# A two-layer hybrid transformer with experts: first-layer expert rows are added to token rows in DRAM instead of by selection matmuls

## What is computed

```python
def expert_choice_ffn(h, w_router, w_gate, w_up, w_down):
    b, n, d = h.shape
    cap = CAPACITY_FACTOR * n // N_EXPERTS
    logits = jnp.einsum('bnd,de->ben', h, w_router).astype(jnp.float32)
    affinity = jax.nn.softmax(logits, axis=1)
    gates, idx = lax.top_k(affinity, cap)
    xs = jax.vmap(lambda hb, ib: hb[ib])(h, idx)
    a = jnp.einsum('becd,edf->becf', xs, w_gate)
    u = jnp.einsum('becd,edf->becf', xs, w_up)
    y = jnp.einsum('becf,efd->becd', jax.nn.silu(a) * u, w_down) * gates[..., None].astype(h.dtype)
    return jax.vmap(lambda yb, ib: jnp.zeros((n, d), yb.dtype).at[ib.reshape(-1)].add(yb.reshape(-1, d)))(y, idx)

# in each layer, after attention
xl = xl + gt_f * expert_choice_ffn(hl, ...)
if not last:
    xc = xc + cgt_f * expert_choice_ffn(hc, ...)
...
return rmsnorm(xl, g_final)
```

## Time and profile before

| | |
|---|---|
| median of three runs | 2272.16 us (2271.99 to 2275.36) |
| the profiled execution | 2279.44 us, span 2277.6 us |
| mean granted TensorE clock | 0.957 |
| TensorE busy | 2057.2 us, 90% of the span |
| VectorE, ScalarE, GpSimd busy | 823.4, 512.1, 124.7 us |
| DMA | 504.67 MB, mean 222 GB/s |

### The profile page before, as it was taken

The page is one execution under the profiler, slowest core; times in us unless marked ns, Lnnn a source line. Parts: engine busy times, 40 slices in busy tenths (PEclk is TensorE's granted clock), DMA queues, the critical chain, the costliest instruction groups (busy, mean ns, idle before and its releaser), DMA issues. The chain is left out here.

```text
span 2277.6 us, 27439 instructions
## 1 busy us (share of the span) xinstructions
PE 2057.2 (90%) x10742; PEld 990.3 (43%) x10742; DVE 823.4 (36%) x2126; ACT 512.1 (22%) x1192; POOL 124.7 (5%) x131
## 2 busy tenths in 40 slices
PE   5999999999988999999999899999999598887875
PEld 3445465655633333333333456455555233332322
DVE  3323256877650111130211431367776402020202
ACT  3211244544430010010100331154444101000001
POOL 1101000000001000000000010100000000000000
PEclk8999979999988999999999899999999799999998
DMA  8841200000079988889889302020003899999995
GB/s 333 304 147 51 55 20 1 1 1 1 19 301 426 405 347 349 354 332 397 339 320 375 114 19 74 1 75 1 1 1 148 340 426 426 427 427 426 427 427 224
DMA packets 87691, 504.67 MB, mean 222 GB/s; under 512 B 10163, under 2 KB 15197, under 8 KB 33293
## 3 DMA queue, kind: packets, MB, share of 16 engines
q1 hardware_dynamic: 82912, 487.00, 53.3%
q0 software_dynamic: 2880, 10.49, 1.3%
q10 hardware_dynamic: 1772, 5.43, 0.6%
HBM read 495.55 MB, written 7.34 MB: 221 GB/s over the span
## 5 line engine op out<-in xcount | busy, mean ns | idle before, releaser
L607 PE MATMUL psS<-arena 128*64 128x512 f32 (+9 forms) x4544 | 1171.8, 560 | 63.2 <-DMA arena<-in_w_up 23.9
L607 PEld LDWEIGHTS psS<-arena 128*64 128x64 f32 (+4 forms) x4544 | 464.0, 161 | 665.0 <-issue 603.5
L610 PE MATMUL psT<-ident,arena 128*128 128x128 f32 (+2 forms) x936 | 155.7, 296 | 68.3 <-DVE arena L1758 24.7
L1906 DVE TENSOR_TENSOR arena<-arena,psS 128x512 f32<-128x512 f32 x32 | 20.6, 684 | 514.7 <-PE psS L607 514.7
L1108 ACT ACTIVATE arena<-psS 128x128 f32<-128x128 f32 (+5 forms) x150 | 57.3, 412 | 581.0 <-PE psS L607 518.1
L610 PEld LDWEIGHTS psT<-ident,arena 128*128 128x128 f32 (+2 forms) x936 | 111.4, 148 | 156.5 <-issue 98.6
L1108 ACT ACTIVATE arena<-psS,nb 128x768 f32<-128x768 f32 (+2 forms) x200 | 159.0, 795 | 79.3 <-DVE nb L1749 77.9
L607 PE MATMUL psT<-arena 128*32 128x512 f32 x1536 | 174.7, 595 | 0.0
L1744 DVE TENSOR_REDUCE mx<-psS 128x1 f32<-128x768 f32 (+2 forms) x200 | 164.9, 824 | 22.9 <-PE psS L607 21.0
L1108 ACT ACTIVATE arena<-psT 128x512 f32<-128x512 f32 (+4 forms) x211 | 108.6, 517 | 225.6 <-PE psT L610 213.7
L607 PE MATMUL psO<-arena 128*64 128x128 f32 (+2 forms) x1600 | 153.2, 299 | 0.0
(11 more groups left out here) (221 smaller groups left out, 1484.9 us busy)
## 6 DMA issues: line engine op xcount, KB each, us to landing
arena<-in_w_gate SPq DMA_DIRECT2D x116, 1024.0 KB, 12.7
arena<-in_w_up SPq DMA_DIRECT2D x116, 1024.0 KB, 12.1
arena<-in_w_down SPq DMA_DIRECT2D x116, 1024.0 KB, 12.3
arena<-in_w_mod SPq DMA_DIRECT2D x40, 1024.0 KB, 9.0
arena<-in_w_in SPq DMA_DIRECT2D x6, 2048.0 KB, 7.9
gtb<-in_w_mod SPq DMA_DIRECT2D x8, 1024.0 KB, 7.2
normed_rows<-arena ACTq DMA_DIRECT2D x10, 512.0 KB, 13.4
arena<-in_w_out SPq DMA_DIRECT2D x8, 512.0 KB, 7.8
```

What stands on the lines that cost most here:

```text
L607: return nc.tensor.matmul(o, lhsT, rhs, start=start, stop=stop)
L610: return nc.tensor.transpose(o, in_, ident[0:n, 0:n])
L1906: last = V.tensor_tensor(ar[:, a:a + 512], ar[:, a:a + 512], bank(2 * g + h), ALU.mult)
```

## The change

In the first layer, the rows of quads 0, 1 and 2 are added to a DRAM copy of X, `summed_rows`; quad 3 and the whole second layer keep `combine`.

- VectorE writes, beside the indices for the gathers, a second form of the picked indices with one expert's rows per column (`idx`).
- SP stores X to `summed_rows` in the first quad, ahead of the first load of stage 6 (3 MiB), and loads it back in the last quad, ahead of the first load of stage 6, after it has waited for all additions.
- GpSimd issues for each of the three quads eight indirect transfers that add rows of `HID` to rows of `summed_rows`: for each expert its 64 latent rows, then its 32 context rows. Each latent one waits for the latent one before (`s_addl`), each context one for the context one before (`s_addc`). They stand ahead of the gather for the quad after next; those of the third quad stand after the last gather.
- ScalarE's silu for group 0 of quad q waits for two latent additions of quad q-1, that for group 1 for four, that for group 2 for the four context additions.
- `selection`, the high and low parts, `combine` and `combined` are left out for quads 0 to 2. The semaphores `yh`, `yl`, `st`, `ce` are counted over the combined quads alone. Three semaphores that were one per layer are shared by both (`mixed`, `Og`, `xg`), with counts that go on.

```diff
+COMBINED = ((NQ - 1,), tuple(range(NQ)))
+SUMS_STORED_AT, SUMS_LOADED_AT = 6, (NQ - 1) * NSTAGE + 6
...
+        sums = nc.dram_tensor("summed_rows", (NTOK, D), f32).ap()
...
+                    if l == 0 and n == SUMS_STORED_AT * QUAD:
+                        sp.wait_ge(z["xr"], TT)
+                        sp.dma_start(sums.rearrange("(t p) d -> p t d", p=P), X[:, :].rearrange("p (t d) -> p t d", t=TT)).then_inc(s_sum, 16)
+                    if l == 0 and n == SUMS_LOADED_AT * QUAD:
+                        sp.wait_ge(s_addl, 16 * QUAD * (NQ - 1))
+                        sp.wait_ge(s_addc, 16 * QUAD * (NQ - 1))
+                        load(X[:, :].rearrange("p (t d) -> p t d", t=TT), sums.rearrange("(t p) d -> p t d", p=P), s_sum)
...
+                def added(q):
+
+                    if q == 0:
+                        pool.wait_ge(s_sum, 16)
+                        pool.wait_ge(z["lgev"], 1)
+                    for e in range(QUAD):
+                        g, p0 = e // 2, e % 2 * CAP_L
+                        pool.wait_ge(z["y"], hidden_tile(l, q, g))
+                        if q or e:
+                            pool.wait_ge(s_addl, 16 * (QUAD * q + e))
+                        nc.gpsimd.indirect_dma_start(
+                            out=sums, out_offset=bass.IndirectOffsetOnAxis(ap=idx[0:CAP_L, q * QUAD + e:q * QUAD + e + 1], axis=0),
+                            in_=ar[p0:p0 + CAP_L, F["HID"] + g * D:F["HID"] + (g + 1) * D], in_offset=None,
+                            bounds_check=NTOK - 1, compute_op=ALU.add).then_inc(s_addl, 16)
+                        p0, c = e * CAP_C, NE + q * QUAD + e
+                        pool.wait_ge(z["y"], hidden_tile(l, q, 2))
+                        if q or e:
+                            pool.wait_ge(s_addc, 16 * (QUAD * q + e))
+                        nc.gpsimd.indirect_dma_start(
+                            out=sums, out_offset=bass.IndirectOffsetOnAxis(ap=idx[0:CAP_C, c:c + 1], axis=0),
+                            in_=ar[p0:p0 + CAP_C, F["HID"] + 2 * D:F["HID"] + 3 * D], in_offset=None,
+                            bounds_check=NTOK - 1, compute_op=ALU.add).then_inc(s_addc, 16)
+
                 for q in range(NQ):
                     if q == 0:
                         pool.wait_ge(z["want"], 2 * l + 1)
-                    elif q == 1:
-                        pool.wait_ge(z["gp"], KD)
+                    elif q == 1 or l == 0:
+                        if q > 1:
+                            added(q - 2)
+                        pool.wait_ge(z["gp"], KD * q)
                     else:
                         pool.wait_ge(z["ce"], (q - 1) * 2 * len(TILES[l]))
...
+                if l == 0:
+                    added(NQ - 2)
...
-                        if st == 0 and q:
+                        if st == 0 and q - 1 in COMBINED[l]:
                             combine(q - 1)
...
-                        if q:
+                        if q and wc and g < 2:
+                            act.wait_ge(s_addl, 16 * (QUAD * (q - 1) + 2 * (g + 1)))
+                        elif q and wc:
+                            act.wait_ge(s_addc, 16 * QUAD * q)
+                        elif q:
                             act.wait_ge(z["ce"], q * NC)
...
-                    for g in range(NX):
+                    for g in range(NX if q in COMBINED[l] else 0):
                         act.wait_ge(z["y"], hidden_tile(l, q, g))
...
+                            V.tensor_scalar(idx[0:CAP_L, 0:NE], bank(4, 0, CAP_L, 0, NE), float(CTX), None, ALU.add)
+                            link(V.tensor_copy(idx[0:CAP_C, NE:2 * NE], bank(4, 0, CAP_C, 32, NE)))
...
-                    dve.wait_ge(z["yh"], hidden_tile(l, q, g))
+                    if q not in COMBINED[l]:
+                        return
+                    dve.wait_ge(z["yh"], split_tile(l, q, g))
...
-                    if q:
+                    if q - 1 in COMBINED[l]:
                         combined(q - 1)
-                    selection(q)
+                    if q in COMBINED[l]:
+                        selection(q)
```

More of the change, by code:

```diff
@@ L365, in backbone_program @@
         s_g = [sem(f"first_rows{i}") for i in range(3)]
+        s_sum, s_addl, s_addc = sem("sums_moved"), sem("latent_rows_added"), sem("context_rows_added")
         s_xd, s_lgx, s_lgxc = sem("rows_stored"), sem("context_logits"), sem("context_logits_copied")
@@ L372, in backbone_program @@
         Z = [sems(l, "sq xn ht htev htevd proj pact pdve dsq bsq bt btev bs bsa bsd kn kpe kt "
-                     "S nb P mixed T PTa PTd O Og mj me gp ge cp ce xg") for l in range(L)]
-        once = {n: sem(n) for n in "open want gd gt gtev rbp rb fg fgev yh yl wb wo lgev pe_ex prb at dup dupT ffn_done xready fxn_sq fxn xr lp st xt xtd lgp lgpc xp done silu prod hp Cn bn qs he y win0 win1".split()}
+                     "S nb P T PTa PTd O mj me gp ge cp ce") for l in range(L)]
+        once = {n: sem(n) for n in "open want gd gt gtev rbp rb fg fgev yh yl wb wo lgev pe_ex prb at dup dupT ffn_done xready fxn_sq fxn xr lp st xt xtd lgp lgpc xp done silu prod hp Cn bn qs he y win0 win1 mixed Og xg".split()}
         for z in Z:
@@ L404, in hidden_tile, with combine_index, split_tile @@
             return l * NQ * (SW[0] // P) + q * (SW[l] // P) + g + 1
+        def combine_index(l, q):
+            return COMBINED[l].index(q)
+        def split_tile(l, q, g):
+            return l * len(COMBINED[0]) * (SW[0] // P) + combine_index(l, q) * (SW[l] // P) + g + 1
         block = ctx.enter_context(nc.Block())
@@ L718, in job @@
                             pe.wait_ge(z["wo"], 80 * (l + 1))
-                        pe.wait_ge(z["Og"], 4 * (i + 1))
+                        pe.wait_ge(z["Og"], 4 * (l * TT + i + 1))
                         for k in range(KD):
@@ L900, in _ @@
                         s0 = i * SLOTS + LAST_SLOT[u]
-                        pe.wait_ge(z["mixed"], v + 1)
+                        pe.wait_ge(z["mixed"], l * TT * TURNS + v + 1)
                         if 8 <= u < 12:
@@ L918, in _ @@
                         if pv >= 4 and (u % 4 == 0 if 8 <= u < 12 else u % 4 == 1):
-                            pe.wait_ge(z["Og"], i * 4 + u // 4)
+                            pe.wait_ge(z["Og"], 4 * (l * TT + i) + u // 4)
                         if 8 <= u < 12:
@@ L1009, in turn_tokens @@
                     take(b)
-                    pe.wait_ge(z["xg"], 16 * NX * q)
+                    pe.wait_ge(z["xg"], 16 * (l * (NQ - 1) * (SW[0] // P) + NX * q))
                     for i in range(NX):
@@ L1026, in combine @@
                 def combine(q):
-                    pe.wait_ge(z["st"], l * NQ + q + 1)
-                    pe.wait_ge(z["yl"], hidden_tile(l, q, NX - 1))
+                    c = combine_index(l, q)
+                    pe.wait_ge(z["st"], l * len(COMBINED[0]) + c + 1)
+                    pe.wait_ge(z["yl"], split_tile(l, q, NX - 1))
                     for n, (t, h) in enumerate(CJ):
@@ L1039, in combine @@
                         last.then_inc(z["cp"], 1)
-                        free[b] = (z["ce"], q * len(CJ) + n + 1)
+                        free[b] = (z["ce"], c * len(CJ) + n + 1)
                 def group(q, st, g):
@@ L1394, in _ @@
                 for n, t in enumerate(tl):
-                    act.wait_ge(z["ce"], (NQ - 1) * NC + 2 * (n + 1))
+                    act.wait_ge(z["ce"], combine_index(l, NQ - 1) * NC + 2 * (n + 1))
                     if n:
@@ L1689, in norm_begin @@
                 def norm_begin(i):
-                    dve.wait_ge(z["Og"], 4 * i + 3)
+                    dve.wait_ge(z["Og"], 4 * (l * TT + i) + 3)
                     link(V.tensor_tensor(tmp[:, 0:256], ar[:, OS:OS + 256], ar[:, OS:OS + 256], ALU.mult))
@@ L1896, in combined @@
                         t, h = CJ[n]
-                        dve.wait_ge(z["cp"], q * len(CJ) + n + 1)
+                        dve.wait_ge(z["cp"], combine_index(l, q) * len(CJ) + n + 1)
                         a = t * D + h * 512
@@ L1954, in _ @@
                 if l < L - 1:
+                    dve.wait_ge(s_sum, 32)
                     combined(NQ - 1)
-                    dve.wait_ge(z["ce"], NQ * len(CJ))
+                    dve.wait_ge(z["ce"], len(COMBINED[l]) * len(CJ))
                     dve.sem_inc(z["xready"], 1)
```

## The result

The changed kernel takes 2248.0 us (2244.9 to 2249.9, four runs) against 2273.8 us before in the same comparison: ratio 0.9883, interval 0.9865 to 0.9901, so 25.7 us faster with an interval of about 22 to 31. The forecast was 30.3 us. The profiled execution took 2244.86 us, the lowest of the four.

What follows compares the result with a forecast made beforehand. TensorE was taken to bound the first layer's expert stage, with the DMA engines close behind. -33.0 + 1.1 + 0.4 + 1.2 = -30.3 us took the median from 2272.2 to 2242 us, range 2237 to 2260.

Steps and rivals of the forecast that it cites:

- What bounds the stage: First layer's expert stage: TensorE sets the time, DMA engines a close second limit; removing three combines takes off 33.0 us.
- Indices: Two small VectorE instructions for the additions' indices, 0.4 us, hidden behind TensorE's late modulation matmuls: cost 0.
- Storing X at 1.1 us: First quad: 7.7 us store on SP's queue against a 6.6 us margin of load 31; bounds 0 and about 5.
- The chain of additions at 0: Linked additions land after 5 to 10 us each; up to 13.6 us delays no silu, so cost 0.
- The slower rival: Additions landing after over 13.6 us stall silu and TensorE in three quads; 2300 at 20 us; chance of slower 0.11.
- Engine time of the additions: DMA engines, quads 1 and 2: 3.7 or 7.4 us per quad, barely hidden; 0.4 us for both, bounds 0 and 4.
- a margin of about 9: Fourth load of a stage: 14.1 us from burst to need, less some 5 us to land.
- B = 5.0: Lag of the DMA queue before X is loaded back in quad 3, forecast at 0.7 to 4.4 us.
- The prediction's 2244 by that rule: Whole kernel: additions with double read traffic take 7.4 us of engines per quad, making the sum 2244 instead of 2242.
- rival B: DMA engines become the bound: additions count double or store and load run slow; most likely near 2246; chance 0.24.
- the likeliest one: Whole kernel: the forecast case, 2242 us, own range 2239 to 2246; chance 0.50 (2239.5 to 2244).
- B's severe form: Store and load of X take 12 us each, adding 4.3 and 4.6 us and as much again: 2256.

Runs made afterwards that it cites:

- the run that waited 0.4 us: Changed kernel with the additions replaced by plain writes over the rows of the DRAM copy, sums left out: 2241.0 us, one profiled run.
- the single chain: Changed kernel with each addition waiting for the one before of either kind, eight in a row instead of two chains of four: 2278.1 us, ratio 1.0018.

## Why the prediction was right, point by point

**What bounds the stage: right.** Removing TensorE's work alone gave 33.0 us, the sum of the rows. The profile after shows the rest of what was foreseen: stage 0 runs into stage 1, the waits stand at stage 6 of the first and of the last quad, the DMA share of the first three quads is 0.98 or more, and no silu is released by a DMA. The waits at stage 4 of quads 1 and 2 were in the sum but not among these signs.

**Indices: right.** Stage 0 began no later for them. TensorE's waits for modulation loads are 7.8 us where they were 7.6, and the last gather's wait was 1.76 us where before it was 1.75.

**Storing X at 1.1 us: 1.8 in the profile, and in part luck.** Place and mechanism as told, the loads of stage 6; group 0, for which I had named no wait, lost 0.2 us too, and each place costs about 0.25 us beyond its idle time. But the waits were 0 to 1.6 us over five runs, by how late the loads were. In the trace of before, the loads issued after stage 2 took up to 14.2 us to land, near the 14.4 of the run that waited 0.4 us. At that lead 1.1 us was thus rather too much, and the 1.8 came with later loads.

**The chain of additions at 0: right.** Landing 8.2 and 6.9 us, inside the forecast 5 to 10 and far from 13.6. The slower rival was put to the test by the single chain: TensorE waited 8.1 and 1.5, 9.5 and 6.8 us, and the time crossed that of before, as the rival's arithmetic of about 10 us a quad says. Two things it had no term for: matmuls run slower behind such waits, 5.7 us in all, and the issue of an adding transfer takes 1.3 to 1.4 us of GpSimd where a gather's takes 1.0.

**Engine time of the additions: the step that was mis-sized.** I bounded it by 3.7 and 7.4 us a quad and took a value between; it is 8.0. With writes, at 3.9, the waits in quads 1, 2 and 3 were gone. The gather, too, takes more than its bytes say. Over the 15 us of the before trace that hold the three for quad 2, q0 has 33.7% of the engines:

```profile
q0 software_dynamic: 432, 1.57, 33.7%
```

5.1 us, not 3.7. With 8.0 and 5.1 the prediction's own formulas give a lag of 8.0 - 3.0 + 5.1 = 10.1 us in quads 1 and 2 against a margin of about 9, so 1.1 us each (measured 0.8 and 0.6, forecast 0.4 for both), and B = 5.0 before the load of X, so 5.0 + 11.5 - 14.1 = 2.4 us (measured 2.8, forecast 1.2). The rule of the Trainium skill that was weighed, "Collectives: The Full Stack", section "The bandwidth ceiling: the fold count and why AG ≠ RS ≠ AR", says that the add of a reduce between cores needs two source reads; the trace agrees in size, 8.0 us adding against 3.9 writing the same rows, and doesn't show the second read. The prediction's 2244 by that rule takes rival B's smaller margins; with the margin of 9 us these 7.4 us would have cost nothing in quads 1 and 2.

**The sum.** -33.0 + 1.8 + 1.4 + 2.8 = -27.0 us against the forecast -30.3: additions and gathers cost 1.4 where 0.4 stood, the load of X 2.8 where 1.2 stood. The rest to the measured 25.7 lies within its interval. The case that came is rival B in its mild form, given 0.24, and not the likeliest one, given 0.50. The measured 2248.0 lies outside the latter's 2239 to 2246 (before, too, took 1.6 us more in this comparison than in the three runs forecast from), and the sign named for B, waits for weights of over 4 us in all, is there with 5.0. B's condition, additions that count double, is what the traces show; its price, 5.1 us of stalls, stands against 6.0. The time stayed in the stated range because that range took in B. The price of B's severe form doesn't add up: 5.1 + 2 x (4.3 + 4.6) = 22.9 us of stalls give 2262, not 2256; nothing of it came.

## What to carry to other kernels

Moving work from a full engine to the DMA queues paid here by the rows removed, 33.0 us, less what the new transfers did to the lead of the loads, 6.0. For each new transfer, work out how far ahead the next load is at that place and how much free engine time follows before the next crowd: the same 3 MiB store cost 0 to 1.8 us at stage 6, 3.2 us more at stage 11 than at stage 8 (535.9 against 532.7), and no wait in its own quad at stage 8. Price an accumulating transfer at twice a plain write (8.0 against 3.9 us for 1.57 MB), and count its chain: four links hid behind four stages of matmuls, eight did not, and took the whole gain.

## What the runs showed that I had not expected

The gathers of 4 KB rows took more engine time than their bytes at 427 GB/s: 5.1 us for 1.57 MB, where 3.7 would be its share, while writes of the same size took 3.9. An addition that ran alone still needed 7.9 us to land for 64 rows (a quarter of a megabyte) and 6.6 for 32, about the same as beside another. And one profile of a kernel gives one lead of its loads: the same store cost nothing or 1.8 us, depending on whether the loads before it took up to 13.7 or 15.7 us to land.
